# Attention in a four-branch hybrid block: the softmax probabilities are scaled by their reciprocal sums in ScalarE copies, one per head, instead of in one VectorE product per round

## The reference, cut to what matters

```python
m = jnp.maximum(jnp.max(s, axis=-1, keepdims=True), sink)
p = jnp.exp(s - m)
p = p / (jnp.sum(p, axis=-1, keepdims=True) + jnp.exp(sink - m))
o = jnp.einsum('bnhgqs,bnshd->bnqhgd', p.astype(v.dtype), vb)
```

## Time and profile before

| | |
|---|---|
| median of 3 runs | 2177.24 us (2174.08 to 2177.93) |
| profiled execution, own time | 2175.79 us |
| its span in the profile | 2173.9 us |
| PE busy | 1803.5 us (83%) |
| DVE busy | 941.3 us (43%) |
| ACT busy | 556.0 us (26%) |

### The profile page before, as it was taken

How to read it: one execution, slowest core, us unless ns; L and a number is a source line. 1 busy time by engine, 2 the same in 40 slices (tenths; PEclk the granted TensorE clock), 3 DMA queues, 4 the chain that set the end, 5 groups by cost and what they waited for, 6 DMA issues and landing times.

```text
span 2173.9 us, 31021 instructions
## 1 busy us (share of the span) xinstructions
PE 1803.5 (83%) x13580; PEld 1235.2 (57%) x13580; DVE 941.3 (43%) x1331; ACT 556.0 (26%) x636; POOL 30.2 (1%) x23
## 2 busy tenths in 40 slices
PE   8999999999999999999999987665656566666665
PEld 7998788888999878888878742121111111111111
DVE  7787578666778658765587520000000000000000
ACT  4555023444356212443463020000000000000001
POOL 0000000000000010000000000000000000000000
PEclk9999999999999999999999999887888888887888
DMA  8443645656543364556644689999999999999997
GB/s 288 160 155 131 243 154 173 194 153 215 193 157 128 145 262 142 168 181 168 207 152 156 272 343 427 427 427 429 429 428 428 428 428 429 429 429 428 427 428 320
DMA packets 189606, 613.29 MB, mean 282 GB/s; under 512 B 8344, under 2 KB 105145, under 8 KB 164281
## 3 DMA queue, kind: packets, MB, share of 16 engines
q1 hardware_dynamic: 186928, 602.04, 71.1%
q10 hardware_dynamic: 2568, 9.63, 1.3%
HBM read 610.60 MB, written 1.05 MB: 281 GB/s over the span
## 4 chain that ended last, share of the span: by engine, by line
PE 50%; DMA 37%; DVE 9%; ACT 3%; issue 1%; ACTq 0%; SPq 0%; DVEq 0%; PEldq 0%
DMA work<-in_w_down 13%; DMA work<-in_w_up 12%; DMA work<-in_w_gate 12%; PE PS L1998 10%; PE PS L1999 5%; PE PS L1902 3%; PE PS L1980 3%; PE PS L1973 3%; PE PS L1975 3%; PE PS L1102 3%; PE PS L1866 2%; DVE ring_low L2740 1%; PE PS L794 1%; PE PS L1118 1%; PE PS L2012 1%
## 5 line engine op out<-in xcount | busy, mean ns | idle before, releaser
L1102 PE MATMUL PS<-work,proj 128*32 128x512 f32 x1024 | 155.4, 741 | 98.4 <-DMA work<-in_w_up 59.2
L1704 DVE TENSOR_TENSOR proj<-proj,PS 128x512 f32<-128x512 f32 x16 | 11.0, 687 | 495.4 <-PE PS L1102 495.4
L1998 PE MATMUL PS<-x_both,high_f 128*128 128x512 f32 x608 | 210.9, 396 | 0.0
L1999 PE MATMUL PS<-x_both,ring_low 128*128 128x256 f32 x704 | 195.7, 278 | 0.0
L1102 PE MATMUL PS<-ring,proj 128*32 128x512 f32 x768 | 118.5, 748 | 84.3 <-DMA ring<-in_w_up 46.1
L2723 DVE TENSOR_TENSOR ring_low<-ring,high_f 128x4096 fp32r<-128x4096 f32 (+1 forms) x38 | 146.8, 3863 | 26.6 <-ACT high_f L2459 26.5
L1102 PEld LDWEIGHTS PS<-work,proj 128*32 128x32 f32 x1024 | 31.2, 123 | 216.5 <-DMA work<-in_w_up 96.9
L2459 ACT ACTIVATE high_f<-ring 128x4096 fp32r<-128x4096 f32 (+1 forms) x38 | 121.1, 3187 | 114.3 <-PE PS L1999 96.3
L1395 ACT ACTIVATE proj<-PS 128x512 f32<-128x512 f32 x16 | 9.6, 597 | 515.5 <-PE PS L1102 515.5
L1999 PEld LDWEIGHTS PS<-x_both,ring_low 128*128 128x128 f32 x704 | 132.3, 188 | 0.0
L1708 DVE TENSOR_TENSOR proj<-PS,xT 128x512 f32<-128x512 f32 x32 | 20.7, 686 | 251.5 <-PE PS L1118 234.9
(11 more groups left out here) (556 smaller groups left out, 3535.6 us busy)
## 6 DMA issues: line engine op xcount, KB each, us to landing
ring<-in_w_in SPq DMA_DIRECT2D x73, 1024.0 KB, 7.2
work<-in_w_gate SPq DMA_DIRECT2D x32, 2048.0 KB, 35.6
work<-in_w_up SPq DMA_DIRECT2D x32, 2048.0 KB, 36.1
work<-in_w_down SPq DMA_DIRECT2D x28, 2048.0 KB, 35.9
ring<-in_w_up SPq DMA_DIRECT2D x25, 2048.0 KB, 35.7
ring<-in_w_gate SPq DMA_DIRECT2D x23, 2048.0 KB, 35.8
ring<-in_w_down SPq DMA_DIRECT2D x22, 2048.0 KB, 36.7
ring<-in_w_ada SPq DMA_DIRECT2D x24, 1024.0 KB, 8.5
```

The costliest lines, as they stand in the source:

```text
L1102: mm = nt.matmul(PS[32 * j:32 * j + 32, 2 + n // 4, :], x(k), w[:, F_E * kk + 512 * j:F_E * kk + 512 * (j + 1)], start=(k == 0), stop=(k = ...
L1998: nt.matmul(PS[:, at + b, :], h[:, c:c + P], both[:, k, :], start=(k == 0), stop=False, skip_group_check=True)
L1999: mm = nt.matmul(PS[:, at + b, 0:T], w[:, c:c + P], both[:, k, 0:T], start=False, stop=(k == kn - 1), skip_group_check=True)
```

## The change: what it does, and the diff

VectorE's product over 1024 columns (L3022) is gone. ScalarE makes the same product in place, one Copy per head with the head's reciprocal sum, a 128x1 operand, as its scale: 8 copies of 128x128 in round 0, 4 copies of 128x256 in each of rounds 1 and 2. They stand behind the first `proj_out` of the round and ahead of `tile_highs` (where there is one) and the second `proj_out`. A new semaphore, `sc_inv`, goes from VectorE's reciprocal to ScalarE; `p_ready`, for which TensorE's transposes wait, now comes from ScalarE's last copy.

```diff
@@ ScalarE, attention(l), in the loop over rounds
                     ins.then_inc(sc_exp, 1)
                     na.activation(SK[:, 0:len(heads)], SK[:, 0:len(heads)], ACT.Exp).then_inc(sc_exp, 1)
                     proj_out(l, 22 + 2 * r, 23 + 2 * r)
+                    act.wait_ge(sc_inv, r + 1)
+                    for n in range(len(heads)):
+                        s = SCO[:, w * n:w * (n + 1)]
+                        ins = na.activation(s, s, ACT.Copy, scale=SUM[:, n:n + 1])
+                    ins.then_inc(p_ready, 1)
                     if r:
                         tile_highs(l, 24 + 2 * r)
                     proj_out(l, 23 + 2 * r, 24 + 2 * r)
@@ VectorE, attention(l), in the loop over rounds
                     dve.wait_ge(sc_exp, 2 * (rnd + 1))
                     link(nv.tensor_tensor(SUM[:, 0:n], SUM[:, 0:n], SK[:, 0:n], ALU.add))
-                    link(nv.reciprocal(SUM[:, 0:n], SUM[:, 0:n]))
-                    nv.tensor_tensor(s, s, wide(SUM), ALU.mult).then_inc(p_ready, 1)
+                    nv.reciprocal(SUM[:, 0:n], SUM[:, 0:n]).then_inc(sc_inv, 1)
                     tile_lows(l, 24 + 2 * rnd)
```

More of the change, by code:

```diff
@@ L438, in build @@
             rhs_ready rhs_out u_ready u_out y_ready y_out s_ready st_ready ln_in ln_ss ln_std ln_rs ln_wide ob_ready
-            att_sq att_ss att_std att_rs att_wide att_qk att_tr att_kv sc_ready sc_max sc_exp p_ready pt_ready pt_out oa_ready oa_out
+            att_sq att_ss att_std att_rs att_wide att_qk att_tr att_kv sc_ready sc_max sc_exp sc_inv p_ready pt_ready pt_out oa_ready oa_out
             rot_ready rot_out vr_ready vr_out dec_loaded rs_ready rs_out oc_psum oc_out oc_sq oc_ss oc_std oc_rs oc_wide oc_ready""".split()
@@ L444, in build @@
          rhs_ready, rhs_out, u_ready, u_out, y_ready, y_out, s_ready, st_ready, ln_in, ln_ss, ln_std, ln_rs, ln_wide, ob_ready,
-         att_sq, att_ss, att_std, att_rs, att_wide, att_qk, att_tr, att_kv, sc_ready, sc_max, sc_exp, p_ready, pt_ready, pt_out, oa_ready, oa_out,
+         att_sq, att_ss, att_std, att_rs, att_wide, att_qk, att_tr, att_kv, sc_ready, sc_max, sc_exp, sc_inv, p_ready, pt_ready, pt_out, oa_ready, oa_out,
          rot_ready, rot_out, vr_ready, vr_out, dec_loaded, rs_ready, rs_out, oc_psum, oc_out, oc_sq, oc_ss, oc_std, oc_rs, oc_wide, oc_ready) = (L[n] for n in names)
@@ L3003, in attention @@
                     s = SCO.rearrange("p (a b) -> p a b", b=w)
-                    wide = lambda a: a[:, 0:n].unsqueeze(2).broadcast_to([P, n, w])
                     mask = con[:, C_BAND:C_BAND + w] if t else con[:, C_CAUSAL:C_CAUSAL + P]
```

## The result

The changed kernel takes 2182.96 us (median of 12 runs, 2182.14 to 2184.80); the kernel before took 2177.28 in 12 runs beside it (2174.08 to 2178.68). The ratio is 1.0029, with an interval of 1.0020 to 1.0037: 5.7 us slower by the medians. A second set of runs of both on another occasion gave 1.0034 (1.0021 to 1.0048).

What follows compares the result with a forecast made beforehand. It took the attention rounds' chain to run over VectorE, then ScalarE's high pieces, with TensorE the bound behind them. 0.56 + 1.60 + 1.60 = 3.76 us a layer, 7.5 for two, on 2177.24 gave 2184.7 us; range 2179.4 to 2188.2.

Steps and rivals of the forecast that it cites:

- Cost of one copy: ScalarE's scaling copies in the attention rounds: eight of 128x128 take 2.42 us, four of 128x256 delay ScalarE by 1.60.
- The middle value between the bounds: Copy price taken between one instruction over 1024 columns (2179.4 us in all) and an Exp with its read (2187.6).
- The rival of cheap copies: Copies run nearer the pace of one instruction, giving 2179.4 to some 2182 us; chance 0.14.
- Round 0: First attention round: VectorE, waiting for the high pieces of block 25, is 0.56 us late instead of 1.15 early.
- Rounds 1 and 2: Later attention rounds: four copies ahead of ScalarE's high pieces make them 1.60 us later each round; removing the product brings nothing.
- Sum: Delay of the attention rounds: 3.76 us for a layer, 7.5 us for two.
- Absorption: Behind round 2 an idle time set by something unmoving, such as a transfer, absorbs the delay; time stays 2177.2; chance 0.07.
- The removal pays: Removing VectorE's product from the chain gains at most 1.15 us a layer, 2174.9 us; chance 0.03 of over 0.2% faster.
- The clock: TensorE's clock falls after six longer waits, costing 1 to 2 us each, giving 2190 to 2196 us; chance 0.03.

Runs made afterwards that it cites:

- e4: The kernel before with VectorE's product left out and nothing in its place, so probabilities go on unscaled; ratio 0.9992 to the kernel before.
- e3: The changed kernel with one copy over all 1024 columns per round instead of eight or four, using the first head's sum; ratio 1.0017 to the kernel before.
- e2: The changed kernel with ScalarE copies in rounds 1 and 2 only, VectorE's product kept in round 0; ratio 1.0032 to the kernel before.
- e6: The changed kernel with the copies moved ahead of each round's first proj_out and its table load; ratio 1.0044 to the kernel before.
- e7: The changed kernel with the copies, then the high pieces of block 24 + 2r, ahead of the first proj_out; ratio 1.0028 to the kernel before.

## Why the prediction was right

The forecast was 2184.7 us, the measurement 2182.96, and the cause is the one that it named. By its steps:

- *Cost of one copy*: 2.42 and 1.70 us for eight and four, measured 2.44 and 1.70. The middle value between the bounds was right. The estimate from the Trainium skill, "ScalarE: Activation LUTs", section "What ACT_TABLE_LOAD costs", was 2.44 and 1.69, and the trace agrees with it. The rival of cheap copies falls.
- *Round 0*: 0.56 us forecast, 0.71 measured, the one term that was off. With the 0.55 us of the later start taken off, the transposes start 1.44 us late (1.42 forecast); the remaining 0.15 are the copy L2581 and the high pieces, 0.09 later than I added up (the eight transposes ahead of them take 1.09 us, 1.03 before), and VectorE's restart, 0.10 us behind `high_w` (173.49 in the old count) rather than 0.03. VectorE's wait there is 2.05 us, not 1.7: before, the low piece started 1.38 us after the reciprocal (165.37 and 166.75), now it starts 0.12 us after it (165.91 and 166.03), so 1.26 went away and not 1.15.
- *Rounds 1 and 2*: 1.60 each forecast, 1.59 and 1.57 measured. VectorE's wait went from 2.10 to 4.95 us (4.85 forecast). TensorE waits 1.24, 0.44 and 0.80 us where 1.4, 0.5 and 0.8 were expected.
- *Sum*: 3.76 us a layer forecast, 3.87 measured, so 7.74 for both, against 7.5. The time grew by 5.7 us by the medians, but the two sets of runs allow 4.4 to 8.1 and 4.6 to 10.4 us, so 7.7 is inside both. How much of the 2 us between is scatter of the last part, whose length varies by more than that among single executions, and how much is a lasting gain somewhere, these runs don't settle.
- *Absorption*: the slip at L2143 is 4.42 us in the first layer (218.50 against 214.08, 0.55 of it from ahead of the stage), 8.66 in the second (743.24 against 734.58) and 8.73 at the experts. Nothing gave it back on the way. In the second pair of traces it is 9.69 there (1311.16 against 1301.47), so one such difference is good to about 1 us.
- *The removal pays*: measured by e4, 0.8 us a layer, where 1.15 was put as the most (and 0.86 expected ahead of e4), and less than the copies cost at the cheapest (e3).
- *The clock*: no fall in the rounds in either trace of the changed kernel. With waits somewhat longer or closer together it can happen (e2, e6, e7), and it costs 0.9 to 1.3 us each time. As a rival it was small in price as well: 1 us a fall, where I took 1 to 2 us in all six rounds.

## What to carry to other kernels

A low busy share doesn't make an engine free in a given stage: ScalarE was 26% busy in the whole, and back to back in just the 4 us (180.3 to 184.1 before) that end with the piece for which VectorE and TensorE both wait. Before moving work, look at what the receiving engine has queued behind the place, and who waits for that, and look whether the giving engine goes on from the place without a wait. When an engine's result is waited for, the cheaper step is often to change its order: here two high pieces moved ahead of a table load and a copy that nobody needed yet brought 5 to 7 us, where the move of work lost 6.

## What the runs showed of the hardware that I had not expected

The granted clock fell for some 3 to 4 us in the middle of a nearly full stretch of TensorE, after waits of 1.21 and 0.80 us 2 us apart (e2), after one of 2.12 us (e7) and after ones of 2.02 and 2.03 us (e6, both layers). In the first layers of e2 and e7, with the same order and nearly the same waits (1.15 and 0.80 us; 2.13 us), it didn't, nor after the waits of 1.70 us in round 2 of e6. So after a wait like these a kernel may or may not have to pay a second price, and two layers of one trace needn't both show it. It shows in no wait of TensorE, only in the granted clock and in the distance between matmuls; another engine's wait for TensorE is then easily put down to the order of the work.
